# TensorE's order in both attention branches: turning or sums ahead of the gate half, values last

## The reference

```python
# branch A, per block of 128 queries, 8 heads
logits = einsum(qa, c_sel) * SCALE + bias          # keys chosen by an index score, causal
probs = softmax(where(valid, logits, -inf))
o = einsum(probs, c_sel)
# branch B, stick breaking
z = einsum(q, k) * SCALE
log_1m = where(mask, log_sigmoid(-z), 0)
after = cumsum(log_1m, reverse=True) - log_1m
a = where(mask, exp(log_sigmoid(z) + after), 0)
o = einsum(a, v)
# then
merged = sigmoid(gate_a) * y_a + sigmoid(gate_b) * y_b   # gates: h @ w, 1024 columns each
```

## Time and profile before

| what | value |
|---|---|
| median of 3 runs | 2391.2 us (2390.89 to 2393.64) |
| the profiled execution, its own time | 2390.79 us |
| its span | 2389.1 us |
| TensorE busy | 2277.5 us, 95% |
| VectorE, ScalarE, GpSimd busy | 38%, 32%, 32% |
| mean granted clock of TensorE | 0.981 of full |
| branch A on TensorE | 179.5 to 262.6 us |
| branch B on TensorE | 263.4 to 359.7 us |

### The profile page before, as it was taken

How to read it: one execution, slowest core, us unless ns; L and a number is a source line. 1 busy time by engine, 2 the same in 40 slices (tenths; PEclk the granted TensorE clock), 3 DMA queues, 4 the chain that set the end, 5 groups by cost and what they waited for, 6 DMA issues and landing times.

```text
span 2389.1 us, 30500 instructions
## 1 busy us (share of the span) xinstructions
PE 2277.5 (95%) x12068; PEld 1731.3 (72%) x12068; DVE 907.0 (38%) x1362; ACT 773.2 (32%) x1154; POOL 771.4 (32%) x414
## 2 busy tenths in 40 slices
PE   7999999889999899899999999999999999999997
PEld 4776667633333479569999999888776686878875
DVE  2576553321111464424750360352000615712712
ACT  3345554211111443653421221423322425212212
POOL 3341226211111134204344444334432044444441
PEclk9899999989999999999999999999999999999999
DMA  4421114568997322102222222233222032323320
GB/s 158 142 88 54 45 45 146 229 226 355 355 376 326 129 87 80 36 10 71 80 80 90 89 86 89 80 98 96 89 76 65 9 97 71 97 88 97 97 88 36
DMA packets 69362, 278.05 MB, mean 116 GB/s; under 512 B 13017, under 2 KB 13145, under 8 KB 56961
## 3 DMA queue, kind: packets, MB, share of 16 engines
q1 hardware_dynamic: 59408, 259.61, 31.3%
q0 software_dynamic: 9552, 16.51, 2.0%
q10 hardware_dynamic: 288, 0.34, 0.1%
HBM read 323.58 MB, written 19.42 MB: 144 GB/s over the span
## 4 chain that ended last, share of the span: by engine, by line
PE 87%; issue 4%; DVE 4%; ACT 2%; POOL 2%; DMA 0%; DVEq 0%; POOLq 0%; SPq 0%; ACTq 0%
PE ps L869 19%; PE ps L886 17%; PE ps L1319 7%; PE ps L1078 5%; PE ps L522 4%; PE ps L1121 4%; PE ps L1341 4%; POOL weights_low L2686 2%; PE ps L1280 2%; PE ps L1105 2%; PE ps L533 2%; PE ps L641 2%; PE ps L1182 2%; PE ps L732 1%; PE ps L852 1%
## 5 line engine op out<-in xcount | busy, mean ns | idle before, releaser
L2686 POOL TENSOR_TENSOR weights_low<-weights,parts 128x1024 fp32r<-128x1024 f32 x250 | 630.6, 2527 | 1096.6 <-ACT parts L1869 1096.6
L869 PE MATMUL ps<-parts 128*128 128x264 f32 x2384 | 450.9, 285 | 8.1 <-DVE parts L2159 6.9
L886 PE MATMUL ps<-parts 128*128 128x512 f32 x1344 | 419.4, 392 | 9.2 <-DVE parts L2159 6.7
L1869 ACT ACTIVATE parts<-weights 128x1024 fp32r<-128x1024 f32 x257 | 269.1, 1054 | 424.4 <-PE ps L869 145.5
L869 PEld LDWEIGHTS ps<-parts 128*128 128x128 f32 x2384 | 375.6, 189 | 8.7 <-issue 8.7
L869 PE MATMUL ps<-parts,weights_low 128*128 128x264 f32 x1120 | 318.7, 285 | 0.0
L886 PEld LDWEIGHTS ps<-parts 128*128 128x128 f32 x1344 | 253.8, 189 | 65.8 <-issue 10.4
L886 PE MATMUL ps<-parts,weights_low 128*128 128x512 f32 x672 | 263.9, 393 | 0.0
L869 PEld LDWEIGHTS ps<-parts,weights_low 128*128 128x128 f32 x1120 | 212.5, 190 | 0.0
L1319 PE MATMUL ps<-area,normed 128*64 128x512 f32 x752 | 171.5, 597 | 1.6 <-DVE normed L2374 1.6
L2159 DVE TENSOR_TENSOR parts<-normed,parts 128x528 f32 (+1 forms) x64 | 152.7, 2387 | 10.1 <-DVE normed L2158 2.7
(11 more groups left out here) (458 smaller groups left out, 3612.3 us busy)
## 6 DMA issues: line engine op xcount, KB each, us to landing
weights<-in_weights SPq DMA_DIRECT2D x283, 512.0 KB, 3.5
area<-in_experts SPq DMA_DIRECT2D x141, 1024.0 KB
area<-pair_rows SPq DMA_DIRECT2D x4, 1024.0 KB, 8.0
bias_scratch<-bias_vector POOLq DMA_DIRECT2D x1, 2560.0 KB, 18.4
residual<-in_x SPq DMA_DIRECT2D x4, 512.0 KB, 6.7
area<-bias_scratch POOLq DMA_DIRECT2D x1, 2048.0 KB, 8.8
token_rows<-area SPq DMA_DIRECT2D x1, 2048.0 KB, 8.7
out_tiles<-residual SPq DMA_DIRECT2D x4, 512.0 KB, 2.8
```

The source lines that it names most:

```text
L869: ins = mm(ps[:, b + h, 0:HALF], wt[:, k], x[m * DT + k][:, HALF * h:HALF * h + HALF], start=m == k == j == 0, stop=m == chunks - 1 and k ...
L886: ins = mm(ps[:, b], wt[:, k], x[:, m * DT + k, first:first + SEQ], start=m == k == j == 0, stop=m == chunks - 1 and k == DT - 1 and j == 2)
L1869: fn(high_slot(n, place), RING[:, n % SLOTS], ACT.Copy).then_inc(S["w_hi"], 1)
L2686: g.tensor_tensor(RING_LOW[:, n % SLOTS], RING[:, n % SLOTS], high_slot(n, place), ALU.subtract).then_inc(S["w_lo"], 1)
```

## The change

TensorE's queue gets another order in both loops; nothing is added or removed, and no other engine's code changes. Branch A: turning, logits two units ahead, gate half, values of the unit before. Branch B: z two units ahead, sums, gate half, values of the unit before.

```diff
@@ pe_dsa @@
                 for u in range(n):
+                    transposed(u)
                     if u + 2 < n:
                         logits(u + 2)
                     gate(u)
-                    transposed(u)
                     if u:
                         values(u - 1)
@@ pe_stick @@
                 for u in range(n):
-                    gate(u)
                     if u + 2 < n:
                         z(u + 2)
                     after(u)
+                    gate(u)
                     if u:
                         values(u - 1)
                 values(n - 1)
```

## The result

The changed kernel takes 2442.6 us (median of 4 runs, 2438.7 to 2445.3) against 2391.9 of the kernel before; the ratio is 1.021, with a 95% interval of 1.0191 to 1.0228. It is 50.6 us slower. (The kernel before has a fourth run here, hence 2391.9 instead of 2391.2.) The forecast was 2435, with a range of 2420 to 2444. The profiled execution of the changed kernel is the longest of its four, 2445.3 us; it spans 2443.6 us, 54.5 more than the profiled one before.

What follows compares the result with a forecast made beforehand. TensorE, busy nearly all the time, was taken to bound the kernel, so a reorder only wins or creates waits. Sum: 2390.8 + 11.6 (branch A) + 22.8 (branch B) + 10.2 (clock) = 2435.4 us; range 2420 to 2444.

Steps and rivals of the forecast that it cites:

- upper bound: Whole kernel: all seven long waits with lost clock and the low part at its full 0.65 us, 2444 us.
- The long waits, branch A: Turning waits 3.0 us at the start for scaling, then 1.9 once and 2.0 three times for ScalarE's copy.
- The short waits, branch A: Turning waits for ScalarE's copy: 1.2 us in the second turn, 0.8 three times, 0.2 to 0.3 three times.
- the low part's lock: Branch A: GpSimd's low part delays VectorE's reduce on the shared port; 0.4 us added where u+2 has two tiles.
- Branch B: Sums wait for the mask behind VectorE's gate copy, plus waits at start and end: 24.5 us, net +22.8.
- The gate half next to values: Branch B: moving a gate next to values instead of z may give or take 0.1 us a turn, up to 1.5.
- The clock: TensorE's clock falls behind six waits of 3.0 to 3.8 us, 1.7 us lost each, 10.2 in all; shorter waits count nothing.
- Full clock behind the waits: Both branches: the waits come but the clock doesn't fall, or falls once; 2425 to 2428 us, chance 0.25.
- VectorE early enough in B: Branch B: the gate tile's copy holds nothing, only A and the two ends of B pay; 2411 us, chance 0.07.
- Faster: Branch A: the chain from logits to copied probabilities fits under one gate half, today's waits go; 2386 us, chance 0.03.
- No effect: TensorE runs what is ready first, so its order doesn't matter; 2391 us, chance 0.02.

Runs made afterwards that it cites:

- ScalarE's copy moved: Changed kernel with ScalarE's copy of unit u ahead of the exponentials of u+2 in branch A, VectorE's order left as it is: 2430.5 us.
- branch B alone: Kernel before with only branch B in the new order, branch A as before: 2425.4 us, ratio 1.014.
- both queues of A moved: Changed kernel with, in branch A, ScalarE's copy ahead of the exponentials of u+2 and VectorE's scaling of u+1 ahead of the maximum of u+2: 2429.4 us.
- the ends moved: Changed kernel with the first turn of branch A and the first and last turns of branch B in the order of before: 2433.5 us.
- The fillers' run: Changed kernel with needless matmuls in the long waits of turns 2, 6, 10, 14 of both branches; attention output not the reference's: 2427.8 us.
- the run that moved it: Changed kernel with VectorE's copy of the gate tile in branch B behind the softplus of the next unit instead of ahead: 2413.9 us.
- the version with mended queues and ends: Changed kernel with ScalarE's copy, VectorE's scaling and gate copy moved, first and last turns in the old order: 2390.3 us against 2392.1 before.

## Why the prediction was right, and where its sizes were off

The direction, the mechanism of the waits and the places of the long ones held, and each was shown by taking it away. The size was 43.8 us forecast (2435 less 2391.2) for 50.6 measured; by the profiled execution 44.6 for 54.5. That 2442.6 lies inside the range is in part luck. The terms named for its upper bound give 2390.8+15+22.8+7x1.7 = 2440.5, not 2444, and those for the lower 2423, not 2420; the clock alone went past the seven spells of 1.7 us that the bound allowed.

**The long waits, branch A.** The forecast was 3.0 at the start, 1.9 in turn 2 and 2.0 in turns 6, 10, 14. Measured: 2.98, 1.72, 1.82, 1.79, 1.82. Right.

**The short waits, branch A.** Forecast 1.2 in turn 1, 0.8 in turns 4, 8 and 12 and 0.25 three times more, 4.4 in all; measured 0.21, three times 0.23 and none, 0.9. Two terms failed. The 0.4 us for the low part's lock in turns 4, 8 and 12 wasn't there: the low part ended before the reduces began (GpSimd 225.95 to 228.31, the reduce of that turn from 229.39). The first turn's gate half ran at half clock behind the 3.0 us wait, 3.95 us, and was so a longer cover for turn 1. So the 15.3 us of waits were 11.1, and the net 11.6 was 7.4.

The size of the lock was misread as well. The prediction says that the rows don't bear out a reduce that loses the whole low part. The trace of the kernel before has three that do, in the turns of the 128x256 reduce, 0.23 us behind the start of a low part: 2.45 us instead of 0.42. The chain for which the prediction added 0.4 us runs over this reduce. VectorE before, then GpSimd before:

```profile
217.01 2.45 DVE L2195 CUSTOM_DVE_ANT_0 area<-area 128x256 f32<-128x256 f32 x1
...
219.38 0.42 DVE L2195 CUSTOM_DVE_ANT_0 area<-area 128x256 f32<-128x256 f32 x1
```

```profile
216.78 2.40 POOL L2686 TENSOR_TENSOR weights_low<-weights,parts 128x1024 fp32r<-128x1024 f32 x1 [8.23 <-ACT parts L1869]
```

In the changed kernel the longest reduce takes 0.78 us. The new order moved the low parts off the reduces, and the prediction had not worked out where they would fall. That the small figure came close is luck. The prediction took a rule from the Trainium skill, "SBUF — State Buffer", section "SBUF: two separate sides": whichever starts second on the shared port blocks until the other's instruction ends. The 2.45 us agree with it.

**Branch B.** Forecast 3.3 at the start, 3.4 three times and 3.8, 1.2 three times, 3.6 at the end: 24.5. Measured 3.54, 3.34, 3.34, 3.67, 3.76, 1.15, 1.15, 1.49, 3.80: 25.2. Right, turn by turn; what was missed is 0.3 us in turns 10 and 12. There the mask took 1.09 and 1.10 us instead of 0.76, beside a subtract of two SBUF operands on VectorE (L2233), which stands in no other middle turn. Turn 10, VectorE then GpSimd:

```profile
360.57 0.69 DVE L2233 TENSOR_TENSOR branch_parts<-area,branch_parts 128x512 fp32r<-128x512 f32 x1
...
360.78 1.09 POOL L2531 TENSOR_SCALAR_AFFINE_SELECT soft_parts<-soft_parts 128x256 fp32r<-128x256 f32 x2 [10.21 <-DVE soft_parts L2243]
```

That may be the shared port once more, with GpSimd as the loser this time; no run took the subtract away to show it. The prediction had looked for it in branch A only. The rule of the Trainium skill, "SBUF — State Buffer", section "SBUF: two separate sides", that whichever starts first holds the port for its whole instruction, agrees with these rows: the subtract starts 0.21 us ahead of the mask.

**The gate half next to values.** The prediction bounded it for branch B, at 0.1 us a turn either way, and put nothing for branch A. In A the gate half is 0.08 dearer (2.94 for 2.86). In B it is 0.1 cheaper, 2.85 for 2.95 from its start to the next instruction, and the whole turn 0.19 cheaper (the z rows of the section on the result): about 3 us saved, twice the bound.

**The clock.** This is the term that was mis-sized: six spells at 1.7 us, 10.2, were forecast. In the profiled execution there are eleven, 58 us at half clock, and they explain most of the 23.6 us that the waits don't (54.5 less 30.9). Two readings failed. First, waits of 1.7 to 1.8 us were counted at nothing, because those of 1.1 and 1.3 before had cost nothing; behind four such waits the clock fell in one execution and behind two in another. Second, show a stage of 3.4 us waits whose spell lasts 3.4 us, and that price was put on every long wait. In the changed kernel the spells behind waits of that length lasted 6.8 in four turns of branch B, and 10.2 at its end. What sets the length stays open. It isn't the work that follows: behind the wait of 3.34 us in turn 2 of branch B, with the same instructions behind it, the clock was low for 6.8 us in the changed kernel and with ScalarE's copy moved, and for 3.4 with branch B alone, with both queues of A moved and with the ends moved.

The fillers' run shows that work in the waits keeps the clock up. The Trainium skill, "TensorE: Matmul & The Clock Gate", section "What's actually happening", says that activity releases the throttle, and that run agrees with it.

The errors in the waits and in the clock partly made up for each other: waits 3.5 us too high, clock up to 13 us too low.

**The rivals.** Full clock behind the waits (2425): refuted by the windows and by the fillers. VectorE early enough in B: refuted by the gate copy's row and the run that moved it. Faster: refuted, though the condition that was named for it (ScalarE copying ahead of the exponentials) is what removes most of the waits of A. No effect: refuted.

## What to carry to other kernels

Before an instruction is moved on one engine, write down what the others have queued between its input and its consumer: here each engine had free time, and most of the 36 us of waits (8.1 and 17.9) came from one copy standing behind work for a later unit (ScalarE, branch A) and another standing ahead of it (VectorE, branch B). Filler work in a software pipeline belongs between an operation and its consumer on the other engines, so an order of TensorE and the orders of ScalarE and VectorE are one design and have to be moved together. On TensorE a wait can cost more than its length; here, by an estimate from the runs, one of 3.3 us with 6.8 us of half clock behind it cost about 6 (3.3 + 6.8x0.42). And take the price of a thing from all its rows, not from one: the rows of one reduce said 0.65 us, three others in the same trace said 2.0.

## What the runs showed of the hardware

- In the two branches of every run the half clock lasted 3.4, 6.8 or 10.2 us at a time. The same wait before the same work was followed by 3.4 us in one execution and by 6.8 in another: turn 2 of branch B (3.34 us), and the start of branch B (3.54 us).
- A wait of 1.7 to 1.9 us ahead of a turning may or may not bring it: 11 of 16 did in the four executions that have such waits (4 of 4, 2 of 4, 2 of 4, 3 of 4). Single waits of 1.5 us and less did not in the changed kernel; two in a row, 1.26 and 0.85, did in one of four executions.
- How much this adds to the spread of the times is not shown: four runs of the changed kernel lie 6.6 us apart, 15 of the kernel before on one chip 5.6.
- The cost of half clock was 0.41 to 0.42 us for each us of it over many spells. Single spells read off two executions give 0.47 and 0.6, with the difference of about 1 us that such executions have anyway.
- 24 needless matmuls of 128 columns, put in a wait of 3.4 us, took 2.90 us and kept the clock at 1.00. They are no remedy: the version with mended queues and ends is 37 us faster than the one with fillers.
- VectorE and GpSimd are slower beside each other: a reduce of 0.42 us took 2.45 and one of 0.68 took 1.33 beside a GpSimd subtract of 2.40, and a GpSimd mask of 0.76 took 1.09 beside a VectorE subtract.
